# Selection of 16 keys out of 64 candidate sums instead of 256, with small tables in PSUM, four buffers for the early expert products, and one-hots compared against an iota in PSUM

## The chip, the cores and the metric

The kernel runs on one core of one Trainium2 chip. The metric is the device time of one execution in microseconds (us); less is better. Engines are written PE (TensorE), DVE (VectorE), ACT (ScalarE), POOL (GpSimd) and SP (SyncE, which here only issues DMAs).

## What is computed

256 tokens of width 1024 go through two blocks. The first has two attention layers (MoBA and NSA) with gated projections; the second has a recurrence beside chunk attention, attention over a memory, and then a product-key expert layer ("PEER") over 128 x 128 = 16384 experts. All of it is float32. The change concerns the expert layer alone:

```python
q = (h @ w_query).reshape(B, S, PEER_HEADS, 2, PEER_KEY_DIM)
sc = jnp.einsum('bshpk,hpnk->bshpn', q, sub_keys)     # 8 heads x 2 halves x 128 scores
v1, i1 = lax.top_k(sc[..., 0, :], PEER_TOPK)          # 16 best of each half
v2, i2 = lax.top_k(sc[..., 1, :], PEER_TOPK)
cand = (v1[..., :, None] + v2[..., None, :]).reshape(B, S, PEER_HEADS, 256)
cand_idx = (i1[..., :, None] * N_KEYS + i2[..., None, :]).reshape(B, S, PEER_HEADS, 256)
top_s, pos = lax.top_k(cand, PEER_TOPK)               # 16 best sums of each head
idx = jnp.take_along_axis(cand_idx, pos, axis=-1)
g = jax.nn.softmax(top_s, axis=-1)
act = jax.nn.gelu(jnp.einsum('td,tkd->tk', xt, expert_u[idx]))
out = jnp.einsum('tk,tkd->td', g * act, expert_v[idx])
```

## The kernel before, in words

It is written by hand for five engines that run side by side; each `engine.wait_ge(semaphore, n)` stands in that engine's own queue, so that everything behind a waiting instruction on the same engine waits too. Fp32 products are made from an upper part and a rest (`whi`, `wlo`) in the fp32r format: ACT writes the upper part, POOL (in the expert loop DVE) subtracts to get the rest, and PE multiplies hi x hi, hi x lo and lo x hi.

The expert layer gathers nothing. It is computed densely: for every second key n (128 of them) all 128 x 256 activations of the experts with that key are made, multiplied with a weight matrix W, and multiplied with the values. W is zero but for the 128 selected experts of a token. Its stages, in order of time:

1. **Scores** (L748 to L762). PE projects the queries and multiplies them with the sub-keys; ACT copies each of 8 pieces to SBUF (L1073); DVE's `top16` (L1566, called at L1588) finds the 16 best values and indices of each row by max8, find-index and match-replace, two rounds, with the indices in `I16u`.
2. **Early products and selection, side by side.** PE makes the activations of `NA` = 30 of the 128 expert tiles ahead of time (L769 to L780), as nothing in them depends on the selection. For each, SP loads 512 KB into one of four slots, ACT writes the upper part (`ahead_hi`, L1075) and later the gelu (L1087), POOL subtracts (L864), and PE does 24 matmuls. `whi` and `wlo` each offer two buffers for this (`i % 2`), so ACT may only write tile i + 2 once PE is done with tile i. Meanwhile DVE, for each half t of 128 tokens (L1590 to L1619), adds 16 x 16 sums per head into `cand` (L1593), runs `top16` over 8 rows of 256 (L1595), splits the position into its two digits by a shift and a mask (L1600 to L1603), and looks up the two key indices: for each digit a one-hot of 128 x 16 against `iota16` (L1607), a multiplication with the table of indices `I16` (L1610) and a sum (L1611). ACT takes the exponentials after early tiles `E_AT` = 15 and 26 (L1090), POOL is not needed by the selection, and PE transposes the first half's result after early tile `SEL0_AT` = 20 (L779) and the second half's after the last early tile (L781).
3. **One-hots and W** (L785 to L800 on PE, L858 to L874 on POOL, L1098 to L1119 on ACT, L1622 to L1650 on DVE). 64 groups of 4 tokens. For group n: DVE writes two one-hots of 128 x 512 by comparing indices with `iota4` (`hot_rows`, L1624: first the one that will carry the gate, then the other); POOL multiplies three of the four tokens' rows with their gates (L859) and ACT the fourth (L1099); PE multiplies the two one-hots, 4 matmuls, into bank 4 + n % 4 (L792); ACT copies 98 columns per token of the bank into W (`w_out`, L1102), one group late; DVE multiplies the other 30 columns per token into the early activations (`weigh_ahead`, L1633), three groups late. Four groups stand ahead of each engine's loop, and the loop runs 15 times over four.
4. **Expert loop** over 98 tiles and the output (L820 to L836). SP loads its first tiles once the last group's matmuls are done (L480).

The lines that the change and the prediction's steps touch, with the few that carry the order:

```python
# L769-779, PE: the early tiles
pe.wait_ge(auhi_ready, i + 1)
h, l = (w[:, i % 2, 0:D].rearrange("p (k n) -> p k n", k=KT) for w in (whi, wlo))
if i == SEL0_AT: transposes("sel0")
# L1078-1080, ACT: when the upper part of tile i may be written
if i < 2: act.wait_ge(proj_done, 2 * NCHUNK - 1 + i)
else:     act.wait_ge(aa_done, i - 1)
# L786-790, PE: what group r waits for
ge(hotA, r + 1); ge(hotG, r + 1); ge(hotB, r + 1)
ge(wt_taken, r + 5); ge(wm_taken, r - 3)
```

`step(...)` on DVE makes the next instruction wait for the end of this one. The rotary stage (L1288 and L1292), which the prediction also reads, is an earlier stage whose DVE operations already have one operand in a PSUM bank.

## Time and profile before

| what | value |
|---|---|
| median of 3 runs | 1860.18 us (1860.07 to 1860.62) |
| the profiled execution, its own time | 1859.88 us |
| its span, first to last instruction | 1857.9 us |
| mean granted clock of PE | 0.934 |
| busy: PE, DVE, ACT, POOL | 1597.2, 1052.9, 829.0, 602.4 us |
| DVE busy, 981 to 1072 us (selection) | 89.20 of 91 us |
| DVE busy, 1072 to 1190 us (one-hots and W) | 116.63 of 118 us |

One execution was traced. A timeline row reads: start, duration, engine, line of the kernel, operation, output <- inputs, partitions x elements, count; "[1.2 <- ACT ...]" is idle time before it and the work that ended the wait. Durations of one instruction include its start-up, and the next instruction of the same engine may start before this one ends: the distance between starts is what a repeated instruction costs. The chain is followed backwards from the last instruction to whatever released each step.

### The profile page before, as it was taken

To read this page: it belongs to the slowest core of one execution; us is meant where nothing else is said; L and a number is where in the kernel's file an instruction comes from. 1 tells how busy PE (TensorE), PEld (TensorE's weight loads), DVE (VectorE), ACT (ScalarE), POOL (GpSimd) and SP (SyncE) were. 2 spreads that over 40 slices of the span, in tenths; PEclk is the share of its full clock that TensorE was granted. 3 is DMA by queue.
4 is the path that set the end of the run, shared out by engine and by line. 5 is a ranking of instruction groups with operands and counts; after the bars stand their busy time and mean duration, and the time that the engine had idled before them with its cause. 6 is when DMAs were issued, how large, how long until landed. Compare 5 with 4: busy or idle time off the path is not lost.

```text
span 1857.9 us, 28590 instructions
## 1 busy us (share of the span) xinstructions
PE 1597.2 (86%) x10659; PEld 1442.0 (78%) x10659; DVE 1052.9 (57%) x2149; ACT 829.0 (45%) x1382; POOL 602.4 (32%) x212
## 2 busy tenths in 40 slices
PE   6987889779786767888799766699999999999996
PEld 6976779756675757887798755599999999999875
DVE  6634347356634673223279999755555555555554
ACT  4553334367332343333344356544444444444443
POOL 5841547710053542663558755300000000000000
PEclk9998879889897888898899989899999999999998
DMA  7630315410032313332324300255555555555453
GB/s 290 233 129 1 136 68 182 159 46 2 1 105 77 114 69 113 132 138 76 112 100 159 102 1 0 89 185 187 192 183 181 182 188 192 184 181 182 164 175 125
DMA packets 36806, 238.44 MB, mean 128 GB/s; under 512 B 4080, under 2 KB 4208, under 8 KB 12144
## 3 DMA queue, kind: packets, MB, share of 16 engines
q1 hardware_dynamic: 36720, 237.27, 36.0%
q8 instruction: 57, 0.93, 0.2%
q14 instruction: 29, 0.24, 0.0%
HBM read 236.21 MB, written 1.05 MB: 128 GB/s over the span
## 4 chain that ended last, share of the span: by engine, by line
PE 54%; DVE 17%; ACT 3%; issue 3%; POOL 1%; DVEq 1%; DMA 0%; ACTq 0%; POOLq 0%
PE bank L816 19%; PE bank L531 10%; PE bank L567 7%; PE bank L564 6%; PE bank L534 5%; DVE raw L1624 3%; PE bank L623 3%; DVE hThi L1230 2%; PE bank L605 2%; DVE arena L1633 1%; DVE arena L1610 1%; DVE arena L1226 1%; POOL wlo L855 1%; DVE arena L1521 1%; ACT whi L913 1%
## 5 line engine op out<-in xcount | busy, mean ns | idle before, releaser
L531 PE MATMUL bank<-hThi,whi 128*128 128x256 f32 x1024 | 252.1, 284 | 5.9 <-ACT whi L1123 5.9
L855 POOL TENSOR_TENSOR wlo<-arena,whi 128x2048 fp32r<-128x2048 f32 x44 | 204.3, 4645 | 149.3 <-ACT whi L913 149.3
L531 PE MATMUL bank<-hTlo,whi 128*128 128x256 f32 x1024 | 251.6, 284 | 0.0
L855 POOL TENSOR_TENSOR wlo<-raw,whi 128x2048 fp32r<-128x2048 f32 x44 | 202.8, 4612 | 112.4 <-ACT whi L913 112.4
L816 PE MATMUL bank<-whi,ghi 128*128 128x512 f32 x512 | 204.2, 399 | 1.5 <-DVE glo L1662 0.3
L531 PEld LDWEIGHTS bank<-hThi,whi 128*128 128x128 f32 x1024 | 196.1, 192 | 10.3 <-issue 6.3
L816 PE MATMUL bank<-whi,glo 128*128 128x512 f32 x512 | 203.0, 396 | 0.0
L816 PE MATMUL bank<-wlo,ghi 128*128 128x512 f32 x512 | 202.0, 395 | 0.0
L531 PEld LDWEIGHTS bank<-hTlo,whi 128*128 128x128 f32 x1024 | 196.4, 192 | 4.2 <-issue 0.2
L913 ACT ACTIVATE whi<-arena 128x2048 fp32r<-128x2048 f32 x44 | 84.3, 1916 | 225.9 <-PE bank L567 146.8
L913 ACT ACTIVATE whi<-raw 128x2048 fp32r<-128x2048 f32 x44 | 84.2, 1914 | 178.0 <-PE bank L567 113.7
L567 PE MATMUL bank<-whi,hThi 128*128 128x256 f32 x960 | 138.9, 302 | 20.8 <-DVE hThi L1230 20.8
L1126 ACT ACTIVATE gact<-bank 128x256 f32<-128x256 f32 x98 | 37.8, 385 | 263.8 <-PE bank L534 263.8
L534 PE MATMUL bank<-hThi,wlo 128*128 128x256 f32 x1024 | 145.3, 285 | 8.4 <-POOL wlo L864 8.4
L1657 DVE TENSOR_TENSOR gact<-gact,arena 128x256 f32<-128x256 f32 x98 | 41.7, 425 | 191.7 <-ACT gact L1126 191.7
L567 PEld LDWEIGHTS bank<-whi,hThi 128*128 128x128 f32 x960 | 131.1, 209 | 24.4 <-DVE hThi L1230 23.5
L534 PEld LDWEIGHTS bank<-hThi,wlo 128*128 128x128 f32 x1024 | 132.7, 193 | 10.0 <-POOL wlo L864 10.0
L567 PE MATMUL bank<-wlo,hThi 128*128 128x256 f32 x960 | 129.1, 289 | 0.9 <-POOL wlo L855 0.9
L567 PE MATMUL bank<-whi,hTlo 128*128 128x256 f32 x960 | 124.9, 283 | 0.0
L567 PEld LDWEIGHTS bank<-wlo,hThi 128*128 128x128 f32 x960 | 123.8, 198 | 1.2 <-POOL wlo L855 1.1
L567 PEld LDWEIGHTS bank<-whi,hTlo 128*128 128x128 f32 x960 | 119.5, 192 | 0.0
L816 PEld LDWEIGHTS bank<-whi,ghi 128*128 128x128 f32 x512 | 96.5, 189 | 28.0 <-DVE wlo L1680 7.4
(225 smaller groups left out, 3188.4 us busy)
## 6 DMA issues: line engine op xcount, KB each, us to landing
raw<-ex_in SPq DMA_DIRECT2D x66, 1024.0 KB, 4.8
raw<-w_in SPq DMA_DIRECT2D x44, 1024.0 KB, 4.8
arena<-w_in SPq DMA_DIRECT2D x44, 1024.0 KB, 4.8
xw<-ex_in SPq DMA_DIRECT2D x32, 1024.0 KB, 4.8
raw<-ex_in SPq DMA_DIRECT2D x50, 512.0 KB, 3.5
xw<-ex_in SPq DMA_DIRECT2D x10, 512.0 KB, 3.4
arena<-frt_in SPq DMA_DIRECT2D x1, 3904.0 KB, 15.0
arena<-tab_in SPq DMA_DIRECT2D x1, 1089.0 KB, 16.3
```

The source lines that it names most:

```text
L531: mm(out, lhs, rhs, start=(k == 0), stop=False)
L534: last = mm(out, lhs, rhs, start=False, stop=(k == len(lo_pairs) - 1))
L564: last = mm(bank[2 * (c % 2) + half][:, T * j:T * j + T], w[:, k, P * j:P * j + P], h[:, k, :], start=first, stop=final)
L567: last = mm(bank[2 * (c % 2) + j][:, UC * half:UC * half + UC], h[:, k, P * j:P * j + P], w[:, k, :], start=first, stop=final)
L605: last = mm(bank[6 + n % 2][:, 0:j["nk"]], j["q"][k], j["k"][k], start=(k == 0), stop=(k == len(j["q"]) - 1))
L623: last = mm(bank[2 + j["number"] % 2][:, dv * j["slot"]:dv * (j["slot"] + 1)], PTsb[n % 2][:, b, :], j["v"][b], start=(b == 0), stop=(b == ...
L816: last = mm(bank[2 * t + h][:, :], g[:, j % 2, tok], w[:, j % 2, at], start=False, stop=(final and i == 2), skip_group_check=True)
L855: G.tensor_tensor(wlo[:, u % 2, :], slots[u % RING], whi[:, u % 2, :], ALU.subtract).then_inc(lo_ready, 1)
L913: A(whi[:, u % 2, :], slots[u % RING], ACT.Copy).then_inc(hi_ready, 1)
L1126: A(gact[:, i % 2, :], bank[4 + i % 2][:, 0:T], ACT.Gelu_apprx_tanh).then_inc(a_gelu, 1)
L1624: V.tensor_tensor(onehot[:, r, s], iota4, index.unsqueeze(2).to_broadcast([P, 4, P]), ALU.is_equal).then_inc(ready, 1)
L1657: V.tensor_tensor(gact[:, i % 2, :], gact[:, i % 2, :], weights, ALU.mult).then_inc(g_ready, 1)
```

## The change

Three things are changed.

**Selection.** Of the 16 x 16 sums of a head only 64 are made: row 0 of the first half with all 16 of the second, rows 1 to 3 with the first 8, rows 4 to 7 with the first 4, rows 8 to 15 with the first one. (The values are sorted, so the 16 largest sums are among pairs whose ranks, counted from 1, have a product of at most 16, and all of these are in.) So `cand` is 4 additions of 128, 192, 128 and 64 elements, and `top16` runs over rows of 64. The position is turned back into the two ranks by 14 small instructions instead of 4. The index table and `iota16` are copied to PSUM (bank 4) and read from there.

**Early products.** The upper part and the rest of an early tile get four buffers each (`ahi`, `alo`, the two halves of the two buffers before); ACT may write tile i + 4 when PE is done with tile i. `E_AT` goes from (15, 26) to (12, 23) and `SEL0_AT` from 20 to 19.

**One-hots.** `iota` is copied to bank 4 once and the one-hots are compared against it there. Products go to banks 5 to 7 in turn instead of 4 to 7. PE therefore waits for ACT's and DVE's reads of group n - 3 instead of n - 4. The loops are four groups ahead and then 5 times over twelve, instead of 15 times over four.

```diff
-E_AT = (15, 26)
-SEL0_AT = 20
+E_AT = (12, 23)
+SEL0_AT = 19
...
-        iota4 = tb("iota", KEEP, keep).unsqueeze(1).to_broadcast([P, 4, P])
+        iota_ps = bank[4][:, 0:P]
+        wbank = bank[5:8]
...
+        cand = KTb.rearrange("p b t -> p (b t)")[:, 0:PH * 64].rearrange("p (h n) -> p h n", h=PH)
+        I16ps, iota16ps, KPS = bank[4][:, 0:256], bank[4][:, 256:272], bank[4][:, 272:400]
...
+        aslots, ahi, alo = ([w[:, i // 2, D * (i % 2):D * (i % 2) + D] for i in range(4)] for w in (raw, whi, wlo))
...
+        def w_groups(engine, group):
+
+            for n in range(4):
+                group(n % 4, n % 3, lambda s_, k: engine.wait_ge(s_, n + k) if n + k > 0 else None, lambda back: (n - back) // 4)
+            with engine.Fori(0, (T // 4 - 4) // 12) as g:
+                for i in range(12):
+                    group(i % 4, (i + 1) % 3, lambda s_, k: engine.wait_ge(s_, g * 12 + (4 + i + k)),
+                          lambda back: bass.ds(g * 3 + (4 + i - back) // 4, 1))
...
+            def w_group(r, b, ge, at):
+                ge(hotA, 1)
+                ge(hotG, 1)
+                ge(hotB, 1)
+                ge(wt_taken, 8 - 2)
+                ge(wm_taken, -2)
                 for j in range(4):
-                    last = mm(bank[4 + r][:, P * j:P * j + P], onehot[:, r, 0, j, :], onehot[:, r, 1, j, :],
+                    last = mm(wbank[b][:, P * j:P * j + P], onehot[:, r, 0, j, :], onehot[:, r, 1, j, :],
                               start=True, stop=True)
...
-                G.tensor_tensor(wlo[:, i % 2, 0:D], aslots[i % 4], whi[:, i % 2, 0:D], ALU.subtract).then_inc(aulo_ready, 1)
+                G.tensor_tensor(alo[i % 4], aslots[i % 4], ahi[i % 4], ALU.subtract).then_inc(aulo_ready, 1)
...
-                if i < 2:
-                    act.wait_ge(proj_done, 2 * NCHUNK - 1 + i)
+                if i < 4:
+                    act.wait_ge(proj_done, 2 * NCHUNK - 1 + i // 2)
                 else:
-                    act.wait_ge(aa_done, i - 1)
-                A(whi[:, i % 2, 0:D], aslots[i % 4], ACT.Copy).then_inc(auhi_ready, 1)
+                    act.wait_ge(aa_done, i - 3)
+                A(ahi[i % 4], aslots[i % 4], ACT.Copy).then_inc(auhi_ready, 1)
...
-            step(V.tensor_copy(I16, I16u))
+            V.tensor_copy(iota16ps, tb("iota16", KEEP, keep))
...
+                V.tensor_copy(I16ps.rearrange("p (b n) -> p b n", n=16), I16u[:, t])
+                for a0, na, nb, at in ((0, 1, 16, 0), (1, 3, 8, 16), (4, 4, 4, 40), (8, 8, 1, 56)):
+                    last = V.tensor_tensor(cand[:, :, at:at + na * nb].rearrange("p h (a b) -> p h a b", a=na),
+                                           vv[:, :, 0, a0:a0 + na].unsqueeze(3).to_broadcast([P, PH, na, nb]),
+                                           vv[:, :, 1, 0:nb].unsqueeze(2).to_broadcast([P, PH, na, nb]), ALU.add)
+                step(last)
+                top16([cand[:, h, :] for h in range(PH)], [TS[:, h, :] for h in range(PH)],
...
-                V.tensor_scalar(K1u, pos, 4, None, ALU.logical_shift_right)
-                step(V.tensor_scalar(K2u, pos, 15, None, ALU.bitwise_and))
-                V.tensor_copy(K1, K1u)
-                step(V.tensor_copy(K2, K2u))
+                V.tensor_scalar(K1u, pos, 3, None, ALU.logical_shift_right)
+                V.tensor_scalar(K2u, pos, 2, None, ALU.logical_shift_right)
+                step(V.tensor_copy(POSf, pos))
+                step(V.tensor_copy(KPS, K1u))
+                V.tensor_copy(K2, K2u)
+                step(V.scalar_tensor_tensor(KPS, POSf, -47.0, KPS, ALU.add, ALU.max))
+                step(V.scalar_tensor_tensor(KPS, K2, -5.0, KPS, ALU.add, ALU.max))
+                step(V.tensor_scalar(K1, KPS, 1.0, -1.0, ALU.max, ALU.add))
+                step(V.tensor_scalar(KPS, K1, 8.0, 8.0, ALU.mult, ALU.add))
+                V.tensor_scalar(K2, K1, 4.0, 24.0, ALU.mult, ALU.add)
+                step(V.scalar_tensor_tensor(KPS, K1, 16.0, KPS, ALU.mult, ALU.min))
+                step(V.tensor_tensor(KPS, K2, KPS, ALU.min))
+                step(V.scalar_tensor_tensor(KPS, K1, 48.0, KPS, ALU.add, ALU.min))
+                step(V.tensor_tensor(K2, POSf, KPS, ALU.subtract))
...
-                                         tb("iota16", KEEP, keep).unsqueeze(1).to_broadcast([P, 128, 16]), ALU.is_equal))
+                                         iota16ps.unsqueeze(1).to_broadcast([P, 128, 16]), ALU.is_equal))
...
+            V.tensor_copy(iota_ps, tb("iota", KEEP, keep)).then_inc(iota_ready, 1)
+            iota4 = iota_ps.unsqueeze(1).to_broadcast([P, 4, P])
```

## Rows read from the trace of the kernel before

**Rows 1.** Busy time by stretch, all engines (columns: stretch, its length, each engine's busy time, clock, DMA).
```profile
981.00:1072.00 91.00, 74.67 (x601) 72.44 (x600) 89.20 (x171) 38.28 (x56) 73.28 (x26) 0.96 0.37 122
1072.00:1190.00 118.00, 75.48 (x512) 64.52 (x512) 116.63 (x189) 78.24 (x127) 70.60 (x64) 0.97 0.00 0
```

**Rows 2.** The chain that ended last, selection to last group (start us, us, what).
```profile
981.89 2.64 DVE arena L1589
...
986.88 2.72 DVE arena L1570 x8
...
1069.08 0.92 PE bank L525 x3
...
1070.68 0.70 DVE raw L1624
...
1188.53 1.14 PE bank L792 x8
```

**Rows 3.** Timeline of all engines, two groups of the one-hot stage.
```profile
1109.84 0.68 DVE L1624 TENSOR_TENSOR raw<-keep,xw 128x512 f32<-128x512 f32 x1
...
1110.09 1.11 POOL L859 TENSOR_TENSOR raw<-raw,xw 128x384 f32<-128x384 f32 x1 [0.72 <-DVE raw L1624]
1110.44 0.39 DVE L1633 TENSOR_TENSOR arena<-bank,arena 128x120 f32 x1
1110.74 1.61 DVE L1624 TENSOR_TENSOR raw<-keep,xw 128x512 f32<-128x512 f32 x2
...
1111.42 1.15 PE L792 MATMUL bank<-raw 128*128 128x128 f32 x8 [0.68 <-POOL raw L859]
1111.89 0.40 ACT L1099 ACTIVATE raw<-raw,xw 128x128 f32<-128x128 f32 x1 [0.17 <-DVE raw L1624]
1111.92 1.11 POOL L859 TENSOR_TENSOR raw<-raw,xw 128x384 f32<-128x384 f32 x1 [0.72 <-DVE raw L1624]
1112.27 0.39 DVE L1633 TENSOR_TENSOR arena<-bank,arena 128x120 f32 x1
...
1112.71 0.84 ACT L1102 ACTIVATE arena<-bank 128x392 f32 x1 [0.41 <-PE bank L792]
```

**Rows 4.** Timeline of POOL and DVE in the first rotary stage.
```profile
39.74 4.65 POOL L855 TENSOR_TENSOR wlo<-raw,whi 128x2048 fp32r<-128x2048 f32 x1 [1.67 <-ACT whi L913]
...
40.49 1.29 DVE L1288 TENSOR_TENSOR bank<-arena,bank 128x512 f32<-128x512 f32 x2
...
41.82 1.29 DVE L1292 TENSOR_TENSOR arena<-bank,gact 128x512 f32<-128x512 f32 x2
```

**Rows 5.** DVE groups by line and shape, 925 to 1072 us.
```profile
L1610 DVE TENSOR_TENSOR arena<-arena 128x2048 f32<-128x2048 f32 x4 | 15.4, 3839 | 0.1
L1607 DVE TENSOR_TENSOR arena<-arena,keep 128x2048 f32<-128x2048 f32 x4 | 13.3, 3337 | 0.1
L1611 DVE TENSOR_REDUCE arena<-arena 128x128 f32<-128x2048 f32 x4 | 9.1, 2286 | 0.1
...
L1570 DVE MAX8 arena<-arena 128x8 f32<-128x128 f32 x32 | 7.0, 281 | 31.6 <-ACT arena L1073 31.4
...
L1570 DVE MAX8 arena<-arena 128x8 f32<-128x256 f32 x16 | 5.4, 413 | 0.1
```

**Rows 6.** Timeline of DVE, end of the first half's index arithmetic.
```profile
1003.31 0.23 DVE L1602 CAST arena<-arena 128x128 f32<-128x128 uint32 x1
1003.45 2.44 DVE L1603 CAST arena<-arena 128x128 f32<-128x128 uint32 x1
```

**Rows 7.** Timeline of POOL, early products.
```profile
1003.32 2.47 POOL L864 TENSOR_TENSOR wlo<-raw,whi 128x1024 fp32r<-128x1024 f32 x1 [0.47 <-ACT whi L1081]
```

**Rows 8.** Timeline of ACT, gelu of tiles 1, 2 and 29 of the early products.
```profile
971.78 0.38 ACT L1087 ACTIVATE arena<-bank 128x256 f32<-128x256 f32 x1 [1.55 <-PE bank L534]
...
974.66 0.38 ACT L1087 ACTIVATE arena<-bank 128x256 f32<-128x256 f32 x1 [1.55 <-PE bank L534]
...
1063.18 0.38 ACT L1087 ACTIVATE arena<-bank 128x256 f32<-128x256 f32 x1 [2.49 <-PE bank L534]
```

More of the change, by code:

```diff
@@ L774, in _ @@
                     pe.wait_ge(aa_gelu, i - 1)
-                h, l = (w[:, i % 2, 0:D].rearrange("p (k n) -> p k n", k=KT) for w in (whi, wlo))
+                h, l = (w[i % 4].rearrange("p (k n) -> p k n", k=KT) for w in (ahi, alo))
                 products(bank[6 + i % 2][:, 0:T], [(h[:, k, :], t[:, k, :]) for k in range(KT) for t in (hThi, hTlo)],
@@ L1099, in gate_row, with w_out, w_group @@
                 A(onehot[:, r, 0, 3, :], onehot[:, r, 0, 3, :], ACT.Copy, scale=gate).then_inc(hotG, 1)
[L1101 to L1117 removed]
+            def w_out(b, to):
+                A(to, wbank[b][:, :].rearrange("p (t n) -> p t n", t=4)[:, :, 0:NL], ACT.Copy).then_inc(wt_taken, 1)
+            def w_group(r, b, ge, at):
+                ge(hot_ready, 1)
+                if isinstance(at(0), int):
+                    gate_row(r, gates[:, r, at(0), 3:4])
+                    if r > 0:
+                        ge(wt_done, 0)
+                        w_out((b - 1) % 3, W4[:, r - 1, at(1)])
+                else:
+                    gate_row(r, gates[:, r, at(0), 3:4].rearrange("p g j -> p (g j)"))
+                    ge(wt_done, 0)
+                    w_out((b - 1) % 3, W4[:, (r - 1) % 4, at(1)].rearrange("p g t n -> p (g t) n"))
+            w_groups(act, w_group)
             act.wait_ge(wt_done, T // 4)
[L1119 removed]
+            w_out((T // 4 - 1) % 3, W4[:, 3, T // 16 - 1])
             def hi_u(i):
```

93 lines of the change are left out of this document (31 added, 62 removed).

## The prediction, made before the change was run

> **What bounds the kernel now.** I read the busy table by stretch first. In the selection, 981 to 1072 us, DVE is busy 89.20 of 91 us; PE is busy for 74.67. In the one-hot stage, 1072 to 1190 us, DVE is busy 116.63 of 118, PE only 75.48 and POOL 70.60 [rows 1]. The chain agrees: DVE's path begins with the cast at 981.89, the first one-hot starts at 1070.68, and the last group's matmuls end at 1189.67, which lets SP load the first expert tiles [rows 2]. So two stretches of DVE, 88.8 and 119.0 us, stand in line, and what either loses comes off the end one for one, until another engine takes over. Nothing before 981 us and nothing in the expert loop is edited.
>
> The timeline then says what DVE's time is made of. The two one-hots of a group take 1.61 us together, and from one `weigh_ahead` to the next it is 1112.27 - 1110.44 = 1.83 us [rows 3]. But one one-hot alone costs 0.60 us, start to next start (1109.84 to 1110.44), and `weigh_ahead` 0.30 (1110.44 to 1110.74). That makes 1.50; 0.33 us is missing. It is the time from the issue of the first one-hot after `weigh_ahead` until POOL's multiplication ends (1110.09 + 1.11 = 1111.20): a comparison with both inputs in SBUF waits for POOL's instruction, whole. The selection shows the same in pure form: a small cast of 0.23 us runs when it starts with POOL's subtraction at 1003.3, and the next, issued 0.14 us later, takes 2.44, up to POOL's end [rows 6, 7]. The 2048-wide operations with two SBUF inputs average 3.84 and 3.34 us, the reduction of the same width, with one, 2.29 [rows 5]. And with one input in PSUM there is no wait: two 512-wide multiplications take 1.29 us a pair, both inside one POOL subtraction that lasts from 39.74 to 44.39 [rows 4].
>
> **Selection, term by term** (both halves together).
> - `top16` on 64 instead of 256 elements. A max8 is 413 - 281 = 132 ns longer for 128 more elements [rows 5], so 192 fewer save 0.198 us, times 8 rows 1.58 us per pass; a pass of max8 costs 2.72 now [rows 2], and I let the find-index and match-replace passes shrink alike. Five passes, two halves: **-15.8**.
> - Look-up against PSUM: four times (3.34 + 3.84) becomes four times 2 x 2.29: **-10.4** [rows 5].
> - The cast of 2.64 us [rows 2] goes; two PSUM copies of 256 and one of 16 elements come, which I put at 1.0 from the 256-wide max8 (0.41) and the small cast (0.23): **-1.6**.
> - The sums. One addition of 2.35 us (from the cast's end at 984.53 to the first max8 at 986.88 [rows 2]) becomes four additions with 512 elements in all, about 0.9 us unobstructed. Both inputs are in SBUF, so each can wait for POOL, and POOL takes 2.4 to 2.5 us per tile with gaps of 0.47 [rows 7]. With four buffers POOL runs without a gap at first: it then takes the lock between any two of DVE's instructions, as it did between the two casts. I reckon three waits in the first half and two, one of them short, in the second: **+8** (ends: -2.9 with no wait; +16.4 with four full waits each).
> - The ranks. Four instructions, 2.9 us with the last one's wait [rows 6], become 14; at 0.14 to 0.31 us each, between the small cast's start to start and a 128-wide operation, they are some 3.8. Five of them are SBUF to SBUF (two shifts, two casts, one multiply-add) and can wait; the first three should fit into a gap, the other two meet POOL: 7.3 us a half, **+8.8** (ends: +1.8; +26).
> - Copy of `iota`: **+0.3**.
>
> Sum -10.7: the first one-hot starts at **1060.0**.
>
> **What is late next.** PE's early tiles run at 974.66 - 971.78 = 2.88 us each [rows 8]: 24 matmuls, PE-bound. Tile 29's gelu would start at 971.78 + 28 x 2.88 = 1052.4 if nothing stalled; it starts at 1063.18 now, because DVE's long SBUF operations and the two exponentials hold POOL and ACT up and two buffers pass it on. DVE now takes the lock only briefly, and four buffers give POOL some 6 us of slack, so I take 1052.8 with the first half's transposes. The second half's must follow: from the start of the second half's transposes at 1069.08 to the first one-hot it is 1.6 us [rows 2], with the copy of `iota` 1.9, so no one-hot before about 1054.7. PE's floor is 5 us below my 1060, so the four buffers by themselves bring nothing as long as DVE is later; without them POOL's stalls could reach PE again. The first half's result is ready at about 1021, before tile 19 ends (1024), and the sums for the exponentials at 998 and 1036, beside gelu 12 (1003) and 23 (1035). SP's tile loads only move earlier, with POOL.
>
> **One-hot stage.** Reading the table from PSUM takes out the 0.33 us wait and I take the PSUM operand's start as free: the pair in rotary is 1.29 us, of which the second starts 0.60 after the first, as in the one-hots [rows 3, 4]. Period 1.51, 64 groups: 64 x 0.32 = **-20.5**. Behind it: ACT needs 0.40 + 0.84 = 1.24, POOL 1.11 and PE 1.15 per group [rows 3]; all fit, ACT with 0.27 to spare. Three banks: PE waits for copy n - 3, and a group's matmuls start 1111.42, its copy ends 1113.55, 2.1 us later against 4.5 us of three periods. `weigh_ahead` of group n - 3 stands behind the one-hots of n on DVE, 0.9 us after the first, and PE waits for it, but for POOL until 1.5 us: nothing. The waits for registers in the loops stay hidden by the same gaps; the longer body only has fewer turns. The last group's pass through POOL and PE is no longer covered as far: +0.3.
>
> Sum: the last group ends at 1060.0 + 64 x 1.51 + 1.9 = 1158.5 instead of 1189.67, 31 us less. The profiled execution took 1859.88 us in all, 0.3 below the median of 1860.18: I say **1829 us**. A measurement of this kernel can tell about 0.2%, 3.7 us, from no change.
>
> **Rivals.**
> - *PE's floor* (0.21). DVE's short operations mostly hit POOL's gaps, the selection ends by 1053, and PE decides: one-hots from 1054.7, 1824 us; at 1.48 a group 1821. For: gaps are known to be used (the cast at 1003.31). Against: POOL is busy 73.28 of 91 us [rows 1].
> - *The lock moves into the short chain* (0.13). Nine lock-taking instructions a half, each waiting nearly a whole POOL operation: the first one-hot stays near 1070, only the one-hot stage gains: 1839, and 1843 if all nine wait. For: [rows 6, 7]. Against: POOL will have finished all 30 tiles by about 1045, and the lock with it. Here the change to 64 sums would not do what it says: fewer elements, but as much time.
> - *PSUM costs a start* (0.08). `weigh_ahead`, which reads PSUM, takes 0.39 us for 120 elements, where the max8 of 128 takes 0.28 [rows 3, 5]; 0.10 more on each of 128 one-hots is 12.8 us: 1842. Against: the rotary pairs [rows 4]; `weigh_ahead` also walks scattered rows of 30. The Trainium skill, in "VectorE: DVE Perf Modes", section on the TRN2 errata, lists 120 cycles plus the elements for PSUM sources and 58 for SBUF sources; its 62 cycles would be an estimated 65 ns, 8.3 us over the one-hots, and about 1837. The trace speaks against it at 512 elements.
> - *A ring takes over* (0.04). ACT's copy and gate alternate, each waiting for someone else; at 1.7 us per group the stage gains 12 less: 1841.
> - *Slower* (0.03). A comparison that reads the same 128 PSUM columns four times over is in no row. If it ran at half speed, 1.13 instead of 0.60, 128 x 0.53 = 68 us would be added: 1897. It decides from 31 / 128 = 0.24 us more per one-hot, 0.84 from start to start. Against: the first rotary multiplication also reads repeated PSUM values at full speed [rows 4].
>
> **How the numbers follow.** The forecast itself gets 0.51. The low end, 1820, is PE's floor with 1.47 to 1.48 us a group; the high end, 1845, takes in the obstructed chain, the dear PSUM start and the ring singly. Beyond it lie two of these together and the slow comparison. Faster by over 0.2%: 0.96; the same: 0.01; slower: 0.03.
>
> **What would show it.** Right: one-hots at 0.60 us start to start with no row of 1.0, `weigh_ahead` to `weigh_ahead` 1.51; passes of max8 over 8 rows of 64 near 1.2 us; multiplications and comparisons of 2048 all at 2.29; PE's early tiles at 2.88 without POOL in its waits; the first one-hot between 1055 and 1065; sums and rank arithmetic with single instructions of 1 to 2.6 us. Wrong: a first one-hot after 1068, a period over 1.6 with DVE waiting for ACT or PE, or an expert loop that does not end the same 668 us after the last group.

## The result and the profile after

The changed kernel takes 1827.71 us (median of 4 runs, 1826.64 to 1829.18) against 1860.4 us for the kernel before, timed on the same chip: a ratio of 0.9823, 95% interval 0.9807 to 0.9838. It is 32.7 us faster. The profiled execution took 1826.83 us, with a span of 1824.9 us against 1857.9.

The busy table by stretch, cut at the first one-hot of the changed kernel and at the start of its last group's last matmuls (columns as in [rows 1]):

```profile
984.40:1059.94 75.54, 71.70 (x594) 71.10 (x592) 73.12 (x191) 35.25 (x52) 54.19 (x23) 0.98 0.40 140
1059.94:1157.00 97.06, 74.52 (x511) 64.52 (x512) 96.08 (x191) 65.94 (x127) 52.99 (x64) 0.96 0.00 1
```

The first stretch starts with the first new copy of the selection and was 88.8 us long before; the second was 119.0. DVE is still the busy engine of both (73.1 of 75.5 us, 96.1 of 97.1), so the time came off the engine that had set the end, as [rows 1] had it. But PE is now busy 71.7 of 75.5 us in the selection: there is little room left below DVE. POOL's busy time in the one-hot stage fell from 71 to 53 us though its work is the same; that is the lock, read from the other side.

The chain that ended last, from the sums to the last group:

```profile
984.90 8.16 DVE arena L1602 x4
993.09 1.12 DVE arena L1577 x8
...
1002.04 2.04 DVE arena L1615
1005.31 1.66 DVE arena L1620
...
1024.66 3.01 DVE arena L1602 x4
...
1057.91 0.91 PE bank L537 x3
...
1156.17 1.14 PE bank L804 x8
```

It runs through the same stations as [rows 2]: DVE, the transposes, DVE's one-hots, the last group's matmuls. The max8 pass that took 2.72 us takes 1.12. New in it are rows that are much longer than their elements ask for: 8.2 us for four additions that make 512 elements together, 2.04 us for one cast of 128. From the last group's end (1157.3) to the end of the span it is 667.6 us, 668.2 before.

The timeline of DVE shows the new rank arithmetic and the first look-up:

```profile
1001.20 0.21 DVE L1611 TENSOR_SCALAR arena<-arena 128x128 uint32<-128x128 uint32 x1
...
1001.71 0.29 DVE L1614 CAST bank<-arena 128x128 f32<-128x128 uint32 x1
1002.04 2.04 DVE L1615 CAST arena<-arena 128x128 f32<-128x128 uint32 x1
1004.01 0.28 DVE L1616 SCALAR_TENSOR_TENSOR bank<-arena,bank 128x128 f32<-128x128 f32 x1
...
1008.19 2.29 DVE L1628 TENSOR_TENSOR arena<-arena,bank 128x2048 f32<-128x2048 f32 x1
1010.51 2.29 DVE L1631 TENSOR_TENSOR arena<-arena,bank 128x2048 f32<-128x2048 f32 x1
1012.83 2.29 DVE L1632 TENSOR_REDUCE arena<-arena 128x128 f32<-128x2048 f32 x1
```

Instructions whose output or one input is in `bank` (PSUM) keep to 0.28 to 0.30 us; the cast from SBUF to SBUF in their midst takes seven times as long. The comparison and the multiplication of 2048, 3.34 and 3.84 us on average before [rows 5], take what the reduction takes.

One group of the one-hot stage, all engines:

```profile
1101.03 0.83 POOL L867 TENSOR_TENSOR raw<-raw,xw 128x384 f32<-128x384 f32 x1 [0.67 <-DVE raw L1648]
1101.37 0.40 DVE L1658 TENSOR_TENSOR arena<-bank,arena 128x120 f32 x1
1101.67 1.28 DVE L1648 TENSOR_TENSOR raw<-bank,xw 128x512 f32<-128x512 f32 x2
1101.86 0.85 ACT L1110 ACTIVATE arena<-bank 128x392 f32 x1 [0.46 <-PE bank L804]
...
1102.10 1.13 PE L804 MATMUL bank<-raw 128*128 128x128 f32 x8 [0.37 <-POOL raw L867]
...
1102.58 0.83 POOL L867 TENSOR_TENSOR raw<-raw,xw 128x384 f32<-128x384 f32 x1 [0.72 <-DVE raw L1648]
1102.87 0.40 DVE L1658 TENSOR_TENSOR arena<-bank,arena 128x120 f32 x1
```

From `weigh_ahead` to `weigh_ahead` it is 1102.87 - 1101.37 = 1.50 us (1.83 in [rows 3]), the pair of one-hots takes 1.28 instead of 1.61, and POOL's multiplication 0.83 instead of 1.11.

DVE's selection can be written as a ledger, start of a step to start of the next, both halves together, from the timelines of the two kernels:

| step | before, us | after, us | difference | predicted |
|---|---|---|---|---|
| casts and copies of the tables | 2.7 | 0.7 | -1.9 | -1.6 |
| sums | 4.6 | 11.4 | +6.8 | +8 |
| `top16` | 30.7 | 14.7 | -16.0 | -15.8 |
| exponentials' subtraction | 1.7 | 1.8 | +0.1 | 0 |
| ranks | 6.0 | 14.0 | +8.0 | +8.8 |
| look-up and its reductions | 38.3 | 27.9 | -10.4 | -10.4 |
| normalisation of the gates | 3.1 | 2.9 | -0.2 | 0 |
| transposes to first one-hot | 1.7 | 2.2 | +0.4 | +0.3 |
| sum | 88.8 | 75.5 | -13.2 | -10.7 |

The predicted terms add up to -10.7 with their signs; the measured ones save 2.5 us more, of which 2.0 are in sums and ranks.

### The profile page after: what moved, and what is told of

Same layout as the page of the kernel before. It is cut to its first block, busy times and chain, and to the rows that moved or that the text cites. A ratio compares the mean times of both kernels' runs of the same rounds, so it can differ in the third digit from the quotient of the medians.

```text
span 1824.9 us, 28509 instructions
## 1 busy us (share of the span) xinstructions
PE 1598.6 (88%) x10659; PEld 1444.9 (79%) x10659; DVE 1016.2 (56%) x2178; ACT 817.3 (45%) x1382; POOL 569.6 (31%) x212
## 4 chain that ended last, share of the span: by engine, by line
PE 55%; DVE 15%; ACT 3%; issue 3%; POOL 1%; DVEq 0%; DMA 0%; ACTq 0%; POOLq 0%
PE bank L824 20%; PE bank L543 10%; PE bank L579 7%; PE bank L576 6%; PE bank L546 5%; PE bank L635 3%; DVE raw L1648 2%; DVE hThi L1237 2%; PE bank L617 2%; DVE arena L1233 1%; PE bank L804 1%; POOL wlo L863 1%; DVE arena L1528 1%; ACT whi L921 1%; DVE arena L1602 1%
## 5 line engine op out<-in xcount | busy, mean ns | idle before, releaser
L543 PEld LDWEIGHTS bank<-hThi,whi 128*128 128x128 f32 x1024 | 195.8, 191 | 10.4 <-issue 6.4
```

The source lines that it names most:

```text
L543: mm(out, lhs, rhs, start=(k == 0), stop=False)
```

## The experiments

All variants start from the changed kernel unless said otherwise. The kernel before, timed beside them, took 1860.6 to 1861.7 us (medians, or the one run beside the two kernels at the end). In the table "start" is where DVE begins its selection work (the first copy or cast behind the last `top16` of the scores), "last product" is gelu 29 on ACT; both and the first one-hot are from the traces. The start wanders between 981.9 and 984.8 us from run to run although nothing ahead of it differs, and the first early gelu moves with it (968.90 us before, 971.40 in the changed kernel), so differences are taken from it. The variants ran on different chips, each with the kernel before beside it; the ratio compares with that.

| kernel | median, us | ratio, 95% interval | start | last product | first one-hot | from start |
|---|---|---|---|---|---|---|
| before | 1860.4 | | 981.9 | 1063.2 | 1070.7 | 88.8 |
| changed | 1827.71 | 0.9823 (0.9807 to 0.9838) | 984.4 | 1055.2 | 1059.9 | 75.5 |
| one-hots' table in SBUF | 1848.86 | 0.9936 (0.9920 to 0.9951) | 982.6 | 1053.4 | 1058.1 | 75.5 |
| one-hots' part alone | 1838.63 | 0.9884 (0.9868 to 0.9899) | 982.5 | 1063.7 | 1071.6 | 89.2 |
| selection's tables in SBUF | 1838.86 | 0.9878 (0.9862 to 0.9893) | 984.7 | 1067.9 | 1073.0 | 88.3 |
| 256 sums | 1825.64 | 0.9810 (0.9795 to 0.9825) | 982.4 | 1054.1 | 1057.7 | 75.3 |
| two buffers | 1823.71 | 0.9801 (0.9788 to 0.9815) | 983.4 | 1055.7 | 1057.1 | 73.8 |
| 256 sums, two buffers | 1829.85 | 0.9833 (0.9820 to 0.9847) | 981.9 | 1056.5 | 1059.3 | 77.4 |
| old places of early work | 1829.84 | 0.9840 (0.9827 to 0.9854) | 984.4 | 1055.3 | 1062.8 | 78.4 |
| sums with PSUM | 1823.31 | 0.9799 (0.9786 to 0.9813) | 983.6 | 1054.5 | 1055.9 | 72.3 |
| sums and ranks with PSUM | 1823.38 | 0.9795 (0.9782 to 0.9809) | 984.8 | 1055.6 | 1057.0 | 72.3 |
| the same, two buffers | 1824.23 | 0.9802 (0.9789 to 0.9816) | 983.3 | 1055.7 | 1057.1 | 73.8 |

**What the table of the one-hots is worth.** The one-hots read their iota from SBUF again; three banks and the unrolled groups stay.

```diff
-            iota4 = iota_ps.unsqueeze(1).to_broadcast([P, 4, P])
+            iota4 = tb("iota", KEEP, keep).unsqueeze(1).to_broadcast([P, 4, P])
```

> The changed kernel, but the one-hots compare against iota in SBUF again; three banks and the loops over twelve stay. Theory (two SBUF inputs wait for POOL's whole instruction): the distance of weigh_ahead to weigh_ahead goes from 1.50 back to 1.83 us, POOL's gate multiplication from 0.83 back to 1.1 us, the stage from 97.4 to 119 us, and the time to about 1849, 21 more than the changed kernel. Rival (three banks or the longer loop body cost or bring something of their own): the stage comes out more than 1 us away from the 119.0 of the kernel before.

Measured: 1848.86 us, 21 us more than the changed kernel. The selection is unchanged (75.5 us), the stage is as long as before (118.95 us against 118.98, first one-hot to last matmul). Its windows and two rows of its timeline:

```profile
1058.10:1176.80 118.70, 74.42 (x511) 64.31 (x512) 117.92 (x191) 78.31 (x127) 71.00 (x64) 0.97 0.00 0
```

```profile
1108.55 1.11 POOL L867 TENSOR_TENSOR raw<-raw,xw 128x384 f32<-128x384 f32 x1 [0.72 <-DVE raw L1648]
...
1109.21 1.60 DVE L1648 TENSOR_TENSOR raw<-keep,xw 128x512 f32<-128x512 f32 x2
```

The pair takes 1.60 us again and POOL 1.11. So the whole gain of the stage is the place of that one operand: three result banks and the longer loop bodies, by themselves, bring nothing that these rows show. POOL's instruction, the same one with the same operands, is 0.28 us shorter as soon as DVE leaves the shared access alone: in [rows 3] it had stood in wait for the second one-hot while its record ran.

**The same part alone, on the kernel before.** The kernel before with the PSUM iota, three banks and unrolled groups; 256 sums, tables in SBUF, two buffers, old places.

```diff
+            V.tensor_copy(iota_ps, tb("iota", KEEP, keep)).then_inc(iota_ready, 1)
+            iota4 = iota_ps.unsqueeze(1).to_broadcast([P, 4, P])
...
-                    last = mm(bank[4 + r][:, P * j:P * j + P], onehot[:, r, 0, j, :], onehot[:, r, 1, j, :],
+                    last = mm(wbank[b][:, P * j:P * j + P], onehot[:, r, 0, j, :], onehot[:, r, 1, j, :],
```

> The kernel before with the one-hots' part of the change alone: their iota in PSUM, three result banks, the unrolled groups; the selection as it was, with 256 sums, its tables in SBUF, two buffers and the early tiles' places as before. My theory: the one-hot stage takes 97 us in place of 119 us and nothing else moves: first one-hot 88 to 90 us behind VectorE's start on the selection, 1838 to 1841 us in all (the time before less 21.6 us). Rival: the two parts are not independent and their gains overlap or help each other; then the time is off that sum by over 2 us, either way.

Measured: 1838.63 us against 1861.44 for the kernel before beside it, 22.8 us less. The selection takes 89.2 us, the stage is as in the changed kernel:

```profile
1071.60:1168.70 97.10, 74.41 (x511) 64.40 (x512) 96.12 (x191) 65.92 (x127) 52.97 (x64) 0.96 0.00 1
```

The changed kernel without its PSUM iota is 11.9 us faster than the kernel before, this one 22.8: together 34.7, against the 32.7 of the whole change. The two parts are independent to within 2 us.

**What the selection's tables are worth.** The cast to an SBUF table and the SBUF iota of 16 are back; 64 sums and four buffers stay.

```diff
-            V.tensor_copy(iota16ps, tb("iota16", KEEP, keep))
+            I16 = tab[:, 1024:1536].rearrange("p (t b n) -> p t b n", t=TT, b=16)
+            step(V.tensor_copy(I16, I16u))
...
-                                         iota16ps.unsqueeze(1).to_broadcast([P, 128, 16]), ALU.is_equal))
+                                         tb("iota16", KEEP, keep).unsqueeze(1).to_broadcast([P, 128, 16]), ALU.is_equal))
```

> The changed kernel with the index table and iota16 of the selection in SBUF again (the one-hots' iota stays in PSUM). Theory: the eight 2048-wide operations wait for POOL again as long as it has tiles, so DVE ends about 10 us later, the cast of 512 costs another 2: time 1836 to 1841; PE's early tiles, with four buffers, are held up by less than 3 us. Rival (the tables do not matter since PE ends the stage anyway): within 3 us of the changed kernel.

Measured: 1838.86 us, 11 us more than the changed kernel, and the first one-hot 12.8 us further from the start. That is nearly all that the selection had gained: without the PSUM tables, but with four buffers, 64 sums leave 88.3 us where 256 sums and two buffers took 88.8. DVE's groups by line and shape, 984 to 1073 us:

```profile
L1631 DVE TENSOR_TENSOR arena<-arena 128x2048 f32<-128x2048 f32 x4 | 15.4, 3843 | 0.1
L1628 DVE TENSOR_TENSOR arena<-arena,keep 128x2048 f32<-128x2048 f32 x4 | 14.1, 3529 | 0.1
L1632 DVE TENSOR_REDUCE arena<-arena 128x128 f32<-128x2048 f32 x4 | 9.1, 2286 | 0.1
L1597 DVE CAST arena<-arena 128x512 f32<-128x512 uint32 x1 | 8.7, 8653 | 0.0
```

Multiplications and comparisons of the look-up take 29.5 us instead of 18.3. The cast, 2.64 us in the kernel before [rows 2], takes 8.65; more of it below. In return the sums fall to 5.24 + 0.88 us. So 6.0 of the 88.3 us are the longer wait of one cast; 64 sums with SBUF tables and two buffers were not run. TensorE's last early tile was expected under 3 us late and is 12.7 us late: TensorE stood 10.4 us in wait for DVE's result at the first half's transposes. DVE still came last, the first one-hot 5.1 us behind gelu 29.

**What 64 sums are worth.** All 256 sums in one addition, ranks by a shift and a mask, as in the kernel before; tables in PSUM and four buffers stay.

```diff
-                for a0, na, nb, at in ((0, 1, 16, 0), (1, 3, 8, 16), (4, 4, 4, 40), (8, 8, 1, 56)):
-                    last = V.tensor_tensor(cand[:, :, at:at + na * nb]...
+                step(V.tensor_tensor(cand, vv[:, :, 0, :].unsqueeze(3).to_broadcast([P, PH, 16, 16]),
+                                     vv[:, :, 1, :].unsqueeze(2).to_broadcast([P, PH, 16, 16]), ALU.add))
```

> The changed kernel with all 256 sums again (one addition of 2048 elements, top16 over rows of 256, four rank instructions); tables stay in PSUM, four buffers stay. Theory: top16 adds 15.8 us to DVE, but the sums give back 11.3 - 4.6 and the ranks 2 x 4.5, as POOL's lock falls on fewer instructions: the first one-hot 0 to 4 us later than in the changed kernel, time 1828 to 1832. Rival (the number of elements decides): 12 to 16 us more, 1840 to 1844.

Measured: 1825.64 us, below the range expected and 2 us less than with 64 sums (the intervals of the ratios overlap). From the start to the first one-hot it is 75.3 us, 75.5 with 64. Its groups of DVE:

```profile
L1601 DVE TENSOR_TENSOR arena<-arena 128x2048 f32<-128x2048 f32 x2 | 7.2, 3578 | 0.0
L1589 DVE FIND_INDEX8 arena<-arena 128x8 uint32<-128x256 f32 x16 | 6.4, 421 | 0.0
...
L1586 DVE MAX8 arena<-arena 128x8 f32<-128x256 f32 x16 | 5.4, 412 | 0.1
...
L1610 DVE CAST arena<-arena 128x128 f32<-128x128 uint32 x2 | 2.5, 1271 | 0.1
```

The passes are back at 0.41 to 0.42 us per row of 256, so the 16 us that `top16` had lost are paid again; the sums take 7.2 us instead of 11.4 and the ranks 3.7 instead of 14.0, both halves together. Of the ranks' 14.0 us some 6.5 are the waits of two instructions a half (2.04 and 1.66 us each), the rest is that there are 14 of them. A quarter of the elements in more instructions, some of which wait for the shared access: with four buffers nothing is left of the gain.

**What four buffers are worth.** Two buffers for the high and low halves of the early products, the waits as in the kernel before.

```diff
-        aslots, ahi, alo = ([w[:, i // 2, D * (i % 2):D * (i % 2) + D] for i in range(4)] for w in (raw, whi, wlo))
+        aslots = [raw[:, i // 2, D * (i % 2):D * (i % 2) + D] for i in range(4)]
+        ahi, alo = ([w[:, i % 2, 0:D] for i in range(4)] for w in (whi, wlo))
```

> The changed kernel with two buffers for the early products instead of four, and ACT's waits as before. Theory (DVE ends the selection, PE's early tiles only stand 2.7 us behind): POOL no longer runs ahead, so the sums find gaps and DVE ends a few us earlier, while the two table loads and DVE's locks reach PE for 1 to 3 us; in all within -2 to +2 us of the changed kernel. Rival (the buffers carry the gain of the stage): 5 us more or worse, with PE's last early tile after 1060.

Measured: 1823.71 us, 4 us less than the changed kernel (within 2 us was expected; the intervals of the ratios overlap), 1.8 us of it between start and first one-hot. POOL's and DVE's timelines of this variant while the sums are taken:

```profile
983.27 2.40 POOL L873 TENSOR_TENSOR wlo<-raw,whi 128x1024 fp32r<-128x1024 f32 x1 [0.47 <-ACT whi L1090]
986.15 2.40 POOL L873 TENSOR_TENSOR wlo<-raw,whi 128x1024 fp32r<-128x1024 f32 x1 [0.48 <-ACT whi L1090]
```

```profile
983.76 4.88 DVE L1603 TENSOR_TENSOR arena<-arena 128x128 f32<-128x128 f32 x4
```

and of the changed kernel:

```profile
966.72 28.65 POOL L872 TENSOR_TENSOR wlo<-raw,whi 128x1024 fp32r<-128x1024 f32 x12 [11.93 <-ACT whi L1089]
995.84 2.40 POOL L872 TENSOR_TENSOR wlo<-raw,whi 128x1024 fp32r<-128x1024 f32 x1 [0.48 <-ACT whi L1089]
```

```profile
984.81 8.24 DVE L1602 TENSOR_TENSOR arena<-arena 128x128 f32<-128x128 f32 x4
```

With four buffers POOL has twelve products to make and makes them without a pause, 2.39 us each. Ends of products fall at 966.72 + k x 2.39: 985.8, 988.2, 990.6 and 993.0; the four additions end at 993.05. One addition gets its turn at each end. With two buffers POOL pauses 0.48 us after each product, in which more than one addition of 0.2 to 0.3 us fits: 4.88 us. For TensorE four buffers do help a little: with two its early tiles take 85.3 us from first to last gelu, with four 83.8, and it waits for POOL 0.6 us in two waits, with four not at all. In the changed kernel that help is idle, as DVE comes last; in this variant the first one-hot stands 1.4 us behind gelu 29, on TensorE's own chain.

**Both undone.** 256 sums and two buffers, the two edits above together; tables stay in PSUM.

```diff
-                for a0, na, nb, at in ((0, 1, 16, 0), (1, 3, 8, 16), (4, 4, 4, 40), (8, 8, 1, 56)):
...
+        ahi, alo = ([w[:, i % 2, 0:D] for i in range(4)] for w in (whi, wlo))
```

> The changed kernel with 256 sums and two buffers: of the three changes, only what moved to PSUM is left (index table, iota16, iota), with the new places of the exponentials. Theory: this is the whole gain. DVE 75 to 77 us from the first PSUM copy to the first one-hot (75.5 in the changed kernel), PE held up 1 to 3 us by the addition of 2048 elements in SBUF: time 1824 to 1828. Rival (64 sums and four buffers bring something together that they do not alone): over 1830.

Measured: 1829.85 us. From start to first one-hot 77.4 us, 2.1 more than with 256 sums and four buffers; both are slightly above what was expected. TensorE waited for POOL 2.4 us in four waits. That wait did not set the end: the first one-hot stands 2.8 us behind gelu 29, double of what it is where TensorE comes last. The 2.1 us are in DVE's rows of the second half's ranks. Here a cast waits for a product of POOL's; with four buffers POOL stood idle for 3.4 us at that moment (1039.78 to 1043.19), as ACT had not written the next upper part. With two buffers, then with four:

```profile
1040.03 2.42 DVE L1612 CAST arena<-arena 128x128 f32<-128x128 uint32 x1
```

```profile
1040.57 0.22 DVE L1611 CAST arena<-arena 128x128 f32<-128x128 uint32 x1
```

So the two edits are not independent: with 64 sums in four additions, four buffers cost about 2 us of trace (4 us of median); with one long addition they bring as much, by where a pause of POOL's falls. 2 to 4 us is near what the intervals resolve; the signs agree in trace and median, the sizes are rough. Read the other way, the table says what 64 sums are worth with two buffers: 1829.85 less 1823.71, 6 us of median with intervals that do not overlap (0.9820 to 0.9847, 0.9788 to 0.9815), and 3.7 us of trace, up to TensorE's chain. With four buffers they bring nothing, with two they do.

**Old places of the early work.** The exponentials after tiles 15 and 26 and the first half's transposes after tile 20, as before.

```diff
-E_AT = (12, 23)
-SEL0_AT = 19
+E_AT = (15, 26)
+SEL0_AT = 20
```

> The changed kernel with E_AT (15, 26) and SEL0_AT 20 as before. Theory: the second exponential falls behind tile 26, its table loads hold the gelu of tile 27 up, which PE needs for tile 29: 0 to 1.5 us, hidden behind DVE's end; DVE reaches its wait for the exponentials at 1022.7 and 1057.6, after them. Within 1 us of the changed kernel. Rival (the places were needed): 3 us more or worse.

Measured: 1829.84 us, an interval that overlaps that of the changed kernel. The first one-hot is 2.9 us further from the start, where under 1 us was expected. Up to the first half's look-up the trace is the same to 0.1 us; then the first half's normalisation takes 2.53 us instead of 1.65 and the second half's four additions 5.0 instead of 3.1. Neither waits for anything that was moved, but POOL's products beside them stand otherwise, and the moved exponential does that. The exponential with its two table loads (2.9 us in all) holds ACT's upper part up, POOL idles for 1.86 us and then, with four buffers, makes four products without a pause. In the changed kernel, then here:

```profile
1011.63 9.66 POOL L872 TENSOR_TENSOR wlo<-raw,whi 128x1024 fp32r<-128x1024 f32 x4 [1.86 <-ACT whi L1089]
```

```profile
1020.30 9.65 POOL L872 TENSOR_TENSOR wlo<-raw,whi 128x1024 fp32r<-128x1024 f32 x4 [1.86 <-ACT whi L1089]
1022.71 2.53 DVE L1636 TENSOR_TENSOR arena<-arena,sc 128x128 f32<-128x128 f32 x1
1025.49 5.01 DVE L1602 TENSOR_TENSOR arena<-arena 128x128 f32<-128x128 f32 x4
```

After tile 12 that stretch falls beside the look-up, whose instructions have a PSUM operand or one input; after tile 15 it falls on the normalisation and the sums. So the new place is worth 2.9 us of trace here, for a reason that neither the prediction nor this expectation named. It is one trace; the medians alone would not show it.

**Taking the lock from the sums.** The second factor of the sums is copied to PSUM (128 elements), so that each addition has one input there.

```diff
+        VPS = KPS.rearrange("p (h n) -> p h n", h=PH)
...
+                step(V.tensor_copy(VPS, vv[:, :, 1, :]))
...
-                                           vv[:, :, 1, 0:nb].unsqueeze(2).to_broadcast([P, PH, na, nb]), ALU.add)
+                                           VPS[:, :, 0:nb].unsqueeze(2).to_broadcast([P, PH, na, nb]), ALU.add)
```

> The changed kernel, with the second values of the sums copied to PSUM first, so that the four additions read one SBUF operand. Theory: the additions go from 8.24 and 3.09 us to 0.9 each, less 0.35 us each for the copy; DVE would be 8.8 us earlier, but the one-hots cannot start before PE's last early tile, whose gelu is 1.4 us before them where PE decides (seen with two buffers): first one-hot 3 us earlier at most, time 1824 to 1825. Rival (DVE alone sets the start): 8 us less, 1819.

Measured: 1823.31 us, 4.4 less than the changed kernel (the intervals of the ratios still overlap slightly) and 3.3 us less of trace. DVE in the sums of the first half and at the end of the selection:

```profile
984.06 0.28 DVE L1602 COPY bank<-arena 128x128 f32<-128x128 f32 x1
984.38 0.88 DVE L1604 TENSOR_TENSOR arena<-arena,bank 128x128 f32<-128x128 f32 x4
...
1051.25 0.55 DVE L1232 COPY xw<-bank 128x384 f32<-128x384 f32 x1
1054.89 0.56 DVE L1232 COPY xw<-bank 128x384 f32<-128x384 f32 x1 [3.08 <-PE bank L538]
```

The same four additions take 0.88 us instead of 8.24, beside a POOL that runs without a pause: their length was waiting, nothing else. DVE ends some 6 us sooner, and now stands 3.08 us idle: the transposes come behind TensorE's early tiles, and the first one-hot follows 1.4 us behind gelu 29 (1054.49 to 1055.90).

**Taking it from the ranks as well.** The temporaries of the ranks are placed so that each step has one side in PSUM, with one instruction recast.

```diff
-                V.tensor_copy(K2, K2u)
-                step(V.scalar_tensor_tensor(KPS, POSf, -47.0, KPS, ALU.add, ALU.max))
+                V.tensor_copy(K2ps, K2u)
+                step(V.scalar_tensor_tensor(K1, POSf, -47.0, KPS, ALU.add, ALU.max))
...
-                V.tensor_scalar(K2, K1, 4.0, 24.0, ALU.mult, ALU.add)
+                step(V.scalar_tensor_tensor(KPS, K1, 4.0, KPS, ALU.mult, ALU.min))
```

> As before, and the rank arithmetic too written so that no instruction behind the first three goes from SBUF to SBUF. Theory: another 3 us per half off DVE, none of it off the time, as PE already decides: the same as with the sums alone, within 1 us. Rival (DVE alone): 14 us less than the changed kernel, 1813.

Measured: 1823.38 us, no further gain. The last reduction of the look-up starts at 1042.9 us instead of 1048.2, DVE then waits 9.0 us for the transposes, and the one-hots start 1.4 us behind gelu 29 again. That is the floor of TensorE.

**The same with two buffers.** The kernel just above, and the edit to two buffers.

```diff
+        ahi, alo = ([w[:, i % 2, 0:D] for i in range(4)] for w in (whi, wlo))
```

> The changed kernel with the second factor of the sums and the temporaries of the ranks in PSUM, and besides with two buffers for the early products in place of four. My theory: VectorE is then free of GpSimd's lock in sums and ranks, and ends its part of the selection well ahead of TensorE; what is left is TensorE's chain of early tiles, so the first one-hot stays at about 1.4 us behind the last early GELU, whatever VectorE does. With two buffers GpSimd can't run ahead, and a tile of TensorE can again wait for a late low half: I expect 84 to 86 us between the first and the last early GELU, and 1823 to 1826 us in all, as with four buffers. Rival: two buffers suffice only where VectorE never holds the lock from GpSimd for longer than a tile; GpSimd then comes 1 to 3 us late again, TensorE with it, and the time is 1826 to 1829 us. Second rival: a GpSimd that can't run ahead takes nothing from VectorE and both gain, 1820 to 1822 us.

Measured: 1824.23 us, 85.3 us between the first and last gelu (83.8 with four buffers), TensorE held up by POOL for about 1 us in two waits, DVE idle for 9.7. As the first theory has it; what four buffers bring once DVE is out of the way is under 1 us of median, less than the intervals tell.

**What a cast waits for.** The 8.65 us of the cast above fit two readings: a turn at each end of a product for each 128 elements, or no turn until POOL pauses. Both kernels keep the tables in SBUF; the first splits the cast in four.

```diff
-            step(V.tensor_copy(I16, I16u))
+            for t, b0 in ((0, 0), (0, 8), (1, 0)):
+                V.tensor_copy(I16[:, t, b0:b0 + 8], I16u[:, t, b0:b0 + 8])
+            step(V.tensor_copy(I16[:, 1, 8:16], I16u[:, 1, 8:16]))
```

> The changed kernel with its tables in SBUF again, and the cast of 512 indices split into four casts of 128. With the one cast it took 8.65 us, up to GpSimd's first pause; GpSimd ran eleven products without a gap, and three ends of products passed during the cast. Theory: a cast whose both sides are in SBUF gets its turn only in a pause of GpSimd, not where one product follows another directly; the first small cast then waits 8 us or so as well, till about 993, and the others follow within the pause or wait for the next: 8.3 to 11 us for the four. Rival: each waits for one product's end, as the four additions of the changed kernel do (8.24 us for four, each end 2.39 us apart); then the first is done after at most 2.6 us and the four together take about 8 to 9 us as well, but in even steps. The single rows tell these apart. The whole time is near 1839 us by either.

```profile
984.97 6.08 DVE L1598 CAST arena<-arena 128x128 f32<-128x128 uint32 x3
990.97 2.44 DVE L1599 CAST arena<-arena 128x128 f32<-128x128 uint32 x1
```

The theory of the pause fell for casts of 128: three took 6.08 us (the shortest 1.35, the others 2.44), the fourth 2.44, one end of a product each. The second kernel splits it in two (1839.28 us in all, 1839.32 for the first, one run each):

```diff
-            step(V.tensor_copy(I16, I16u))
+            V.tensor_copy(I16[:, 0], I16u[:, 0])
+            step(V.tensor_copy(I16[:, 1], I16u[:, 1]))
```

> As the kernel with four casts, but with two casts of 256 elements each. One cast of 512 took 8.65 us; four of 128 took 8.5 us in steps of about 1.4, 2.4, 2.4 and 2.4 us, each up to the end of a product of GpSimd's. First theory: a cast moves about 128 elements per turn and then lets GpSimd in; a cast of 256 needs two turns: some 3.8 us for the first (1.4 + 2.4) and 4.8 us for the second. Second theory: a cast wider than 128 gets its turn only in a pause of GpSimd: about 8.4 us for the first, under 0.5 us for the second. Third: a cast of any width waits for one product's end, and the 8.65 us were an accident: 1.4 us and 2.5 us. The whole time is 1835 to 1840 us by all three.

Its timelines of DVE and POOL:

```profile
983.90 8.50 DVE L1597 CAST arena<-arena 128x256 f32<-128x256 uint32 x1
992.32 0.28 DVE L1598 CAST arena<-arena 128x256 f32<-128x256 uint32 x1
```

```profile
966.21 26.04 POOL L872 TENSOR_TENSOR wlo<-raw,whi 128x1024 fp32r<-128x1024 f32 x11 [11.93 <-ACT whi L1089]
992.46 2.40 POOL L872 TENSOR_TENSOR wlo<-raw,whi 128x1024 fp32r<-128x1024 f32 x1 [0.21 <-ACT whi L1089]
```

The first cast of 256 let three ends of products pass and got through in POOL's first pause, 992.25 to 992.46; the second ran in 0.28 us. So in these traces a cast of 256 or 512 elements waits for a pause, one of 128 only for an end. It is one record for each width (four for 128). And it holds for casts: in the kernel with 256 sums and four buffers an addition of 2048 elements, both inputs in SBUF, got its turn at the first end of a product (983.8), while POOL went on without a pause until 1002.3:

```profile
982.81 2.99 DVE L1601 TENSOR_TENSOR arena<-arena 128x2048 f32<-128x2048 f32 x1
```

```profile
964.71 37.59 POOL L872 TENSOR_TENSOR wlo<-raw,whi 128x1024 fp32r<-128x1024 f32 x15 [11.94 <-ACT whi L1089]
```

So width alone is not the reason; why wide casts are passed over is open.

## Why the prediction was right

**The bound.** DVE set the end in both stretches, and what it lost came off one for one: 13.3 us of selection and 21.6 of one-hot stage (119.0 to 97.4 us, first one-hot to last matmul) make 34.9; the later start of the selection in this run takes 2.5 of it, the expert loop's end gives 0.6 back: 33.0 us of span.

**The one-hot stage** (forecast 98.5 us, measured 97.4; period 1.51 and 1.50). The reasoning from [rows 3, 4] held: 0.33 us per group was a wait for POOL's instruction, and one PSUM operand takes it out. The experiment that puts this operand back gives the 21 us back. Nothing else came late: ACT at 0.40 + 0.85, PE at 1.13. The step on POOL was off: I took 1.11 us, it is 0.83, with no effect on the time since POOL is not last.

**`top16` and the look-up** (-15.8 and -10.4 forecast, -16.0 and -10.4 measured). Both came from groups of the trace that held nothing but the instruction itself. The PSUM comparison over a repeated table runs at 2.29 us for 2048 elements and the pair of one-hots at 1.28, so neither of the rivals on dear or slow PSUM reads came to pass. The Trainium skill, in "VectorE: DVE Perf Modes", in its section on the TRN2 errata, lists 62 cycles more for an instruction with a PSUM source than for one with SBUF sources; these rows of 512 and 2048 elements don't show them.

**Sums and ranks** (+8 and +8.8 forecast, +6.8 and +8.0 measured). The mechanism was right and the sizes somewhat high. In the first half's sums all four additions waited, one more than reckoned; in the second the wait was shorter. The cast and the multiply-add of the ranks waited 1.7 and 1.4 us a half, as forecast the two of five that did.

**The coincidence.** The first one-hot was forecast at 1060.0 and came at 1059.9. The selection gained 2.5 us more than forecast and started 2.5 us later than in the profile of before; the start wanders by that much. The agreement of the absolute number is luck; that of the terms is not. Against the profiled execution the sum was 1828.7 us (1859.88 less 31.2) and the run took 1826.8: 1.1 us of the difference lie in the one-hot stage, 0.6 in the expert loop.

**The rivals.** "PE's floor" was priced at 1824 us. It was not reached, by 3.3 us (gelu 29 plus 1.4 us would have been 1056.6), but the variants that free the sums from the lock end on it, at 1823.3. The forecast of gelu 29 itself, 1052.8, was met but for the later start (1055.24). "The lock moves into the short chain" was half true from the start: sums and ranks are in the forecast's sum with +16.8, measured +14.8, part waits and part more instructions, and nearly use up what 64 sums save.

**What the forecast missed.** It says that four buffers "by themselves bring nothing as long as DVE is later". Beside the four additions they cost, 1.8 us in the trace: they let POOL run without a pause, and a POOL without a pause admits one short DVE instruction per product where one with pauses admits several. The text had the mechanism (it charged the sums for it) but not the conclusion that two buffers would be faster. It gave the new places of the exponentials no term either; that they keep POOL's second stretch without a pause off the sums (2.9 us in the trace with the old places) was luck. It also left unsaid what its own terms say, -15.8 + 8 + 8.8 = +1.0: that 64 sums bring nothing in this surrounding. The kernel with 256 sums confirms it, and those with two buffers show that it is the surrounding: there they bring 3.7 us of trace.

**The best variants.** The sums with one PSUM factor (1823.31 us) or two buffers (1823.71) are 37 us faster than the kernel before. Against the changed kernel their medians are 4 us lower and their traces 3.3 and 1.8 us shorter; the intervals of the ratios overlap slightly. Below that lies TensorE's chain of early tiles. Whether some of these tiles could run in the one-hot stage, where TensorE is busy 74.5 of 97 us, was not tried.

## What to carry to other kernels

When two engines share an access, count the instructions that take it as well as the elements: four additions that make 512 elements together cost 8.2 us beside a busy GpSimd, and 0.9 us with one operand in PSUM. Move small constant tables and short-lived temporaries to PSUM first; a cut in the arithmetic that is paid for with more instructions may bring nothing as long as some of these wait. Giving a neighbour more buffers so that it can run ahead also takes away the pauses in which the bounding engine got its turns, at the start and after each delay that it catches up on, so look at who fills the gap, and at what it falls on, before adding slack.

## What the runs showed of the hardware

- GpSimd's record includes its wait for the shared access: its multiplication of 384 elements takes 0.83 us beside comparisons with a PSUM input and 1.11 beside comparisons with both inputs in SBUF.
- The turns are whole instructions, and a waiting VectorE addition gets in at an end of a GpSimd instruction even if the next is ready: four additions of 64 to 192 elements ended with four ends of products, 2.39 us apart, and one of 2048 elements got in at the first. The Trainium skill, in "SBUF — State Buffer", section "Who interferes with whom", says that whoever issues first holds the shared pair for its whole instruction, that a VectorE instruction with two SBUF inputs contends with a GpSimd one that reads SBUF, and that one with at most one SBUF input, outside the 2-port perf modes, does not; the rows of additions and one-hots agree (8.24 against 0.88 us, 1.60 against 1.28 us a pair).
- One SBUF input alone is no guarantee: a cast of 128 elements from SBUF to SBUF took 2.04 us beside GpSimd and the multiply-add 1.66, while a cast of the same size from SBUF to PSUM, just before, took 0.29 with a GpSimd product under way (1001.61 to 1004.01).
- Casts from SBUF to SBUF of 256 and 512 elements got no turn at three such ends and took 8.5 and 8.65 us, up to the first pause of 0.2 us, while casts of 128 got a turn at each end. How long a wide cast would stand beside a GpSimd that never pauses was not tried.
- Of PSUM as a source VectorE shows no price here: the 512-wide comparisons follow each other at 0.60 us with their table in PSUM (two from 1101.67 to 1102.87), as with it in SBUF where nothing holds them up (1109.84 to 1110.44 in [rows 3]), and a 2048-wide one takes 2.29 us, like the reduction from SBUF.
